# Value projection of an attention layer: tile by tile with both weight pieces held, chained start-up transfers, and parallel loads of the bias table

## The reference, cut to what matters

```
hp = modulate(rms_norm(xp, norm_g[l, 0]), sh1c, sc1c)
q, k, v = jnp.split(h @ w_qkv, 3, axis=-1)
s_loc = einsum(q, k) * scale + bias      # 2-D neighbourhood, bias from rpb
p = softmax(concatenate([s_loc, s_ctx]))
o = p[local] @ v + p[context] @ v_ctx
```

## Time and profile before

| | us |
|---|---|
| runs, median (lowest to highest) | 2704.92 (2704.63 to 2833.44) |
| profiled execution, its own time | 2705.91 |
| its span, slowest core (2) | 2704.4 |
| spans of the 8 cores | 2690.0 to 2704.4 |
| TensorE busy | 2466.1 (91%) |
| VectorE / ScalarE / POOL busy | 1150.4 / 1036.4 / 299.1 |

### The profile page before, as it was taken

How to read it: one execution, slowest core, us unless ns; L and a number is a source line. 1 busy time by engine, 2 the same in 40 slices (tenths; PEclk the granted TensorE clock), 3 DMA queues, 4 the chain that set the end, 5 groups by cost and what they waited for, 6 DMA issues and landing times.

```text
span 2704.4 us, 41883 instructions; the slowest of 8 cores (2690.0 to 2704.4 us)
## 1 busy us (share of the span) xinstructions
PE 2466.1 (91%) x14955; PEld 1081.2 (40%) x15184; DVE 1150.4 (43%) x1552; ACT 1036.4 (38%) x1571; POOL 299.1 (11%) x323
## 2 busy tenths in 40 slices
PE   2888889999999978999999888899999997799998
PEld 1322224444444433444443222344444453344443
DVE  2344445323325665323244445453232656732333
ACT  4455555302224356302254555551031435630224
POOL 1122210000000030000002222000000002100000
PEclk8999979999999988999999999899999997899999
DMA  9754534555534202555448434155553331122322
GB/s 210 157 74 69 69 54 67 93 95 94 94 63 89 59 1 40 103 103 99 78 73 152 56 55 55 20 89 100 97 94 63 61 60 29 32 47 48 59 51 94
DMA packets 136506, 205.99 MB, mean 76 GB/s; under 512 B 73136, under 2 KB 83376, under 8 KB 135536
## 3 DMA queue, kind: packets, MB, share of 16 engines
q0 software_dynamic: 107824, 158.16, 38.0%
q1 hardware_dynamic: 28480, 45.14, 5.1%
HBM read 322.89 MB, written 31.46 MB: 131 GB/s over the span
## 4 chain that ended last, share of the span: by engine, by line
PE 77%; DVE 6%; issue 6%; ACT 5%; DMA 5%; SPq 0%; DVEq 0%; POOL 0%; ACTq 0%; POOLq 0%
PE pp L654 23%; PE ps L654 19%; PE pp L677 6%; PE ps L884 5%; PE pp L1271 3%; PE pp L1003 3%; PE ps L1028 3%; PE ps L677 2%; PE ps L1271 2%; PE pp L1398 2%; PE pp L1237 2%; DVE scr L976 2%; PE ps L582 2%; PE ps L1037 1%; ACT scr L1021 1%
## 5 line engine op out<-in xcount | busy, mean ns | idle before, releaser
L723 DVE TENSOR_TENSOR big<-big 128x512 bf16<-128x512 f32 x384 | 265.7, 692 | 414.5 <-ACT big L721 414.5
L654 PE MATMUL ps<-hTs,ring 128*128 128x512 bf16 x1488 | 338.4, 382 | 13.8 <-ACT hTs L632 8.8
L654 PE MATMUL pp<-hTs,ring 128*128 128x512 bf16 x1520 | 342.9, 380 | 1.9
L654 PE MATMUL pp<-big,ring 128*128 128x512 bf16 x1362 | 304.9, 379 | 2.7 <-ACT big L721 1.2
L419 POOL DMA_DIRECT2D ring<-wall x140 | 99.0, 707 | 1772.1 <-PE ps L654 512.1
L721 ACT ACTIVATE big<-ps 128x512 f32<-128x512 f32 x190 | 113.2, 596 | 471.9 <-PE ps L654 465.1
L575 ACT ACTIVATE scr<-xTs 128x512 bf16<-128x512 f32 x216 | 133.5, 627 | 336.0 <-DVE xTs L693 276.9
L693 DVE SCALAR_TENSOR_TENSOR xTs<-pp,mod,xTs 128x512 f32<-128x512 f32 x156 | 116.7, 750 | 330.6 <-PE pp L654 239.2
L976 DVE TENSOR_TENSOR scr<-pp,scr 128x768 f32<-128x768 f32 (+2 forms) x192 | 174.7, 911 | 141.9 <-PE pp L1009 70.1
L721 ACT ACTIVATE big<-pp 128x512 f32<-128x512 f32 x194 | 115.4, 596 | 296.1 <-PE pp L654 293.1
L884 PE MATMUL ps<-hTs,ring 128*128 128x512 bf16 x666 | 196.7, 390 | 31.3 <-DVE big L902 9.5
(11 more groups left out here) (117 smaller groups left out, 2704.1 us busy)
## 6 DMA issues: line engine op xcount, KB each, us to landing
ring<-wall POOLq DMA_DIRECT2D x140, 1024.0 KB, 10.8
vo<-big SPq DMA_DIRECT2D x48, 256.0 KB, 6.2
kTo<-big SPq DMA_DIRECT2D x48, 256.0 KB, 2.1
scr<-rpbp POOLq DMA_DIRECT2D x64, 128.0 KB, 3.5
scr<-big SPq DMA_DIRECT2D x128, 54.0 KB, 3.8
xTs<-xT SPq DMA_DIRECT2D x3, 2048.0 KB, 18.7
yT<-scr SPq DMA_DIRECT2D x24, 256.0 KB, 2.1
big<-ckT POOLq DMA_DIRECT2D x2, 512.0 KB, 8.9
```

The source lines that it names most:

```text
L654: ins = e.matmul(ps[pi][:, :], lhsT=w[:, kc, fc * fw:(fc + 1) * fw], rhs=src[:, kc, t * 512:(t + 1) * 512], start=(kc == 0), stop=(kc == n ...
L723: P.op("dve", lambda e: e.tensor_tensor(out=hid[:, hc, t * 512:(t + 1) * 512], in0=ta[:, :], in1=ta[:, :], op=ALU.mult), reads=[ta_r], wri ...
```

## The change

- In layer 0, x tile 2 is issued once x tile 1 has landed (before: piece 3). Piece 5 (second value half) is issued once x tile 1 has landed, piece 6 (query/key) once piece 5 has landed; before, neither had such a wait.
- The value stage runs over tiles first and over the two pieces inside a tile. Both pieces are held until tile 2 and given back after their last blocks.
- In layer 0 the squares of tiles 1 and 2 are written in two lots (five and three chunks), in the first piece of tile 0 and in the second piece of tile 1, each lot ahead of a block's copies; the sums follow two blocks and one block later.
- The bias table has a dependence record and a semaphore for each quarter, so the four transfers do not wait for each other. `scr_begin` and `load_T(0)` move to the start of the last four blocks, `mask_T(0)` behind the stage.

```diff
+    later = {}
     def load_piece():
-              ring_sem[s], writes=[ring_r[s]])
+              ring_sem[s], writes=[ring_r[s]], extra=later.get(n, []))
...
-            extra=[[], [(ring_sem[2], 16)], [(ring_sem[0], 32)]][t])
+            extra=[[], [(ring_sem[2], 16)], [(sem_x[1], 16)]][t])
+    later[5] = [(sem_x[1], 16)]
+    later[6] = [(ring_sem[2], 32)]
...
-            Tsem.extend(P.new_sem(f"T{l}_{n}") for n in range(2))
+            for ap, r in Tb:
+                parts = [r] + [Res(f"Tp{k}", init=scr.inherit) for k in range(3)]
+                scr.live.extend(parts[1:])
+                Tp.append(parts)
+            Tsem.extend([P.new_sem(f"T{l}_{n}_{k}") for k in range(4)] for n in range(2))
...
-                        Tsem[hp % 2], writes=[Tt_r])
+                        Tsem[hp % 2][2 * par + rl], writes=[Tp[hp % 2][2 * par + rl]])
...
-        for j in range(2):
-            s = use_piece("v", l, j)
-            for b in range(12):
-                t = b // 4
-                if l == 0 and j == 0 and b in (0, 4):
-                    ensure_h(b // 4)
-                    norm_whole(b // 4 + 1)
-                if b % 4 == 0:
-                    ensure_h(t)
+        vslots = [use_piece("v", l, j) for j in range(2)]
+        for t, j in [(t, j) for t in range(NT) for j in range(2)]:
+            s = vslots[j]
+            if j == 0:
+                ensure_h(t)
+            if (t, j) == (2, 1):
+                scr_begin()
+                load_T(0)
+            for b in range(4 * t, 4 * t + 4):
+                if l == 0 and (t, j) in ((0, 0), (1, 1)) and b % 2 == 0:
+                    for c in range(5) if b % 4 == 0 else range(5, 8):
+                        norm_chunk(ctx0, c, t + 1, 2 if c < 5 else 1)
...
-            done_piece()
-            if j == 0:
-                scr_begin()
-                load_T(0)
-                mask_T(0)
+            if t == 2:
+                done_piece()
+        mask_T(0)
```

More of the change, by code:

```diff
@@ L775, in attn_layer @@
         rcp = wr[:, 0:1024].bitcast(F32)
-        zb, pT, Tb = [], [], []
+        zb, pT, Tb, Tp = [], [], [], []
         st_sem = [P.new_sem(f"st{l}_{n}") for n in range(4 + 2)]
@@ L805, in load_T @@
         def load_T(hp):
-            Tt, Tt_r = Tb[hp % 2]
+            Tt = Tb[hp % 2][0]
             for par in range(2):
@@ L813, in load_T @@
                         out=Tt[64 * rl:64 * rl + 64, par, :].rearrange("p (o q) -> p o q", o=16), in_=src),
-                        Tsem[hp % 2], writes=[Tt_r])
+                        Tsem[hp % 2][2 * par + rl], writes=[Tp[hp % 2][2 * par + rl]])
         def mask_T(hp):
-            Tt, Tt_r = Tb[hp % 2]
+            Tt, tp = Tb[hp % 2][0], Tp[hp % 2]
             v = Tt[:, :, :].rearrange("p h (o q) -> p (h o) q", o=16)
@@ L820, in mask_T @@
                 out=v, in0=v, in1=V("cmask", 64).unsqueeze(1).to_broadcast([128, 32, 64]), op=ALU.add),
-                reads=[Tt_r, vecs_r], writes=[Tt_r])
+                reads=tp + [vecs_r], writes=tp)
         load_ctx()
-        for j in range(2):
-            s = use_piece("v", l, j)
-            for b in range(12):
-                t = b // 4
-                if l == 0 and j == 0 and b in (0, 4):
-                    ensure_h(b // 4)
-                    norm_whole(b // 4 + 1)
-                if b % 4 == 0:
-                    ensure_h(t)
+        vslots = [use_piece("v", l, j) for j in range(2)]
[10 more added lines that the diff above has]
+                        norm_chunk(ctx0, c, t + 1, 2 if c < 5 else 1)
                 pi = next_ps()
@@ L978, in add @@
                     op=ALU.add),
-                    reads=[ps_r[2 * pp], ps_r[2 * pp + 1], Tt_r], writes=[z_r])
+                    reads=[ps_r[2 * pp], ps_r[2 * pp + 1]] + tp, writes=[z_r])
             b.add = add
```

## The result

Five runs of each kernel stand side by side; three of the changed kernel's, in which one die stood at a lower clock, and one of the other's (2833.44 us) are left out of the ratio. It is 1.0070, with an interval of 1.0048 to 1.0092. The changed kernel is slower, by some 19 us; the forecast was 2702.6 and the range ended at 2715. The profiled execution took 2722.09 us, its slowest core (6) 2720.6.

What follows compares the result with a forecast made beforehand. TensorE, 77% of the chain, was taken as the bound. Gains of 1.1 us (layer 0 stage), 0.9 and 0.3 (layer 2) took 2.3 off 2705.9, giving 2703.6; less 1.0 for the runs' median, 2702.6, range 2689 to 2715.

Steps and rivals of the forecast that it cites:

- The transfers, start: Layer 0: with x tile 2 issued later, piece 4 lands and the first value block starts at 52 us, bounds 51 to 55.1.
- the second of two waits: Layer 0's first value block at 55.24 us also waits for seven sums of tile 1, ending at 55.25.
- Piece 5: Layer 0's second value piece, chained to x tile 1, lands about 62.5 us, some 10.5 after piece 4, wanted after four blocks.
- The one large hole: Layer 0 value stage: TensorE waits 7.7 us once, replacing holes of 4.8 and 4.6; bounds 5 to 10.
- the schedule by hand: Layer 0, from the start of tile 1's second piece: copies, squares, Ln, Exp and normalisation add up to 16.5 us.
- the 60.1 of the sum: Layer 0's value stage lasts 60.1 us, ending at 112.1 against 113.2, a gain of 1.1 us.
- The table: Bias table at the value stage's end: mask ends 14.8 us after it in layer 0 (now 14.8), 15.5 in layer 2 (15.8).
- Rival C: Later table load decides: mask 24.8 us after the stage, 9 to 10 later per layer, 2723 in all; chance 0.18.
- What holding both pieces does: Layer 2's value stage: second piece lands at 1404.7 us, wanted at 1408.2, so holding both costs nothing, 3.5 of cover left.
- the stage of layer 2: Layer 2's value stage: the wait of 0.93 us goes, so it ends at 1443.0 instead of 1443.9.
- the attention loop: Fourteen table loads lose their chain there; gain taken as nothing, bounds 0 and 5.8 us per layer.
- nothing here reaches 2%: Whole kernel: no case reaches 2%, 54 us, about what a measurement can tell from no change.

Runs made afterwards that it cites:

- e4: Kernel before, with x tile 2 waiting for x tile 1 instead of piece 3: piece 4 landed at 53.4 us for 54.1, first value block at 57.5.
- e1: Changed kernel without the added waits of pieces 5 and 6: piece 5 landed at 62.0 us, layer 0's value stage ended at 122.3.
- e3: Changed kernel with tile 2's squares moved to tile 1's first piece: layer 0's value stage ended at 112.0 us; ratio fell by 0.0032.
- e7: e5 plus e3's edit, piece 5's wait removed, piece 6 waiting for x tile 2: layer 0's value stage ended at 110.9 us.
- e8: Kernel before, with only a dependence record and semaphore per table quarter added: mask ended 5.9 and 8.3 us after the stage (layers 0, 2).
- e9: Changed kernel with both next ring pieces made to wait for the third key copy: ratio 0.9999 to the kernel before.
- e5: e2 with both ring-piece issues written behind the query/key groups, without a real wait: first addition 20.3 us after the stage in layer 0.
- e2: Changed kernel with the table loaded ahead of the last eight value blocks, not four: mask 5.3 us, first addition 18.4 after the stage; total unmoved.

## Why the prediction was wrong, step by step

By the prediction's sum the first addition of layer 0 comes at some 127.0; it came at 141.2. Of the 14.2, 9.5 are the stage (end at 112.1 forecast, 121.6 measured) and 4.7 the table. Put on the forecast as an estimate, either alone would have stayed within 2715 (2712.1 or 2707.3), and both together do not (2716.8).

**The transfers, start.** I took 52 for the first block; it was 52.7. The reason given was half wrong: e4 shows that x tile 2's place alone moves piece 4 by 0.7 us. By elimination (e1, e4) the larger part is that the sums left the front of the stream, which the prediction named as the second of two waits and then did not price.

**Piece 5.** "It would only have queued behind piece 4 in any case", so the prediction had it land at about 62.5 and put its wait at nothing. It landed at 67.3, and TensorE waited 2.0 to 6.4 us, 3.9 in the median. The step took the wait for x tile 1 to be free. e1, without the wait, has 62.0: my figure was right for the kernel without the edit. With it the piece is issued when piece 4 has all but landed (50.84 and 51.2 on core 6) and starts level with x tile 2 and the first stores.

**The one large hole.** 7.7 us forecast, 6.8 to 8.1 on seven cores, 10.1 on the eighth. That the hole is right is in part luck, for the stretch that it ends is not: from the start of tile 1's second piece to tile 2's first block the schedule by hand gives 16.5 us, and the median is 20.4. What the schedule lacked were stores: VectorE's copies wait for them, and late copies made the sums' hole of up to 3.9. These two steps, 3.9 each, are most of the 8.8 us by which the stage, 68.9 long, missed the 60.1 of the sum. Of the 11.6 us that the stage grew, e3 gives back 9.6 and e7 2.5 more.

**The table.** The sum took 10.3 us for the ring piece and 1.9 for each of the four quarters behind it, 7.6 in all, so a mask at 14.8 after the stage. Measured in the median: 11.0 for the piece, 11.0 from its landing to that of the last quarter, mask end 19.5 after (on core 6 13.9, 11.1 and 22.9). So the term that was too small is the quarters. The 1.9 came from single quarters, each right behind a piece; four released together take longer, and e8 shows it in the middle of the stage too, so neither the second piece nor the key stores are needed for that.

Rival C had this mechanism, at a chance of 0.18. Its price of 9 to 10 us in each layer did not hold: layer 0 has 4.7 in the median, layer 2 nothing, for there the kernel before was already at 19.4 in the median. I had read core 2 alone, which stands at 15.8, and so saw a table 3.6 us earlier than most cores have it.

**What holding both pieces does.** The prediction asked whether the second piece would be there in time and called the rest free. There is a cost at the other end: both slots come free within 7 us of each other at the stage's end, so two new pieces of 1 MB meet the last stores, the key stores and the table. e9 takes that away and is faster than the changed kernel by 0.7%. But in layer 2 the kernel before waits as long, so this is a price of the change in layer 0 only; the larger part of the loss, 8.0 of 12.7 us, lies in the stage, where e3 and e7 find it.

**Right:** the stage of layer 2 (41.6 for 42.4; 0.9 forecast), the attention loop (264.5 for 265.7 in layer 0, 253.4 for 252.8 in layer 2), and that nothing here reaches 2%.

## What to carry to other kernels

Releasing a buffer is issuing a transfer: when an edit moves the place where a ring slot comes free, look at what else is on the DMA engines there, stores above all, and hold the load back by a wait on the work it should follow; a line moved down in an idle queue's list moves nothing (e5 against e9). Remove a wait, and look for the next one at the same spot before pricing the gain: here the mask hid a key store, and time came only when both were gone (e2, e9). Read a stage on all cores; the slowest core of one run is not the typical one at each step.

## What the runs showed of the hardware that was not expected

Four transfers of 128 KB, read in rows of 64 float32 values (256 bytes) and issued 0.8 us apart, land within 3.3 to 4.0 us each with little else in flight and took 17.2 to 21.9 behind one ring piece and beside 256 KB stores, so the same work is worth 6.4 or some 24 us by its company alone. With stores but no piece ahead (e2) they took 3.3 to 11.7, and with a piece and stores in the middle of the stage (e8) 12.6 to 21.5, so most of the delay comes only with a piece ahead. But the last quarter lands some 11 us after that piece, and why is open.

The Trainium skill, "DMA: Bandwidth & Descriptors", section "Queues, rings and completion order", says that each engine takes its queues in turn, packet by packet. Small packets on POOL's queue would then lose against the large packets of the stores on SP's. That would fit these times, but no run here takes the stores away and leaves the piece, so it is not shown.
